# Token lists of experts 12 to 31 read from a table in DRAM, empty slots left out of the scatter-add, four more ring places ahead of the expert loop, another order in the last norm

## What is computed

```python
logits = xt @ w_router + b_router
top_val, top_idx = lax.top_k(logits, TOP_K)          # TOP_K = 4 of 32
gate_w = jax.nn.softmax(top_val, axis=-1)
h = clamped_swiglu(xe @ w_gate[e] + b_gate[e], xe @ w_up[e] + b_up[e])
y = h @ w_down[e] + b_down[e]                        # for the tokens of expert e
out = zeros.at[token].add(y * gate_w)
x2 = layer_norm(DEEPNORM_ALPHA * x1 + out, ln2_g, ln2_b)
```

## Time and profile before

| | us |
|---|---|
| median of 3 runs | 1449.98 |
| lowest, highest | 1448.16, 1451.69 |
| the profiled execution | 1448.46 |
| its span | 1445.9 |

### The profile page before, as it was taken

One profiled execution on the slowest core, in us unless ns is written; L12 is line 12 of the kernel. 1 busy time (PEld: TensorE's weight loads), 2 busy tenths in 40 slices (PEclk: granted clock), 3 DMA queues, 4 the chain that ended last, 5 costly groups with the idle time before them and its releaser, 6 DMA issues.

```text
span 1445.9 us, 37854 instructions
## 1 busy us (share of the span) xinstructions
PE 1390.0 (96%) x16642; PEld 939.8 (65%) x16642; DVE 468.0 (32%) x891; ACT 325.3 (22%) x669; POOL 116.1 (8%) x122
## 2 busy tenths in 40 slices
PE   7999999998999999999999999999999999999991
PEld 6767776565566666666666666666666666666660
DVE  3335665374323222222222223222222222222224
ACT  4544566131111111111121111111111121111114
POOL 1022000001100000000000000000000001000000
PEclk9999999998999999999999999999999999999995
DMA  8211041727999999999999999999999999999964
GB/s 264 74 49 59 1 151 63 272 102 295 404 394 397 400 392 397 399 400 397 402 399 398 394 392 400 398 398 386 396 397 392 400 391 400 391 392 389 395 269 145
DMA packets 78565, 463.94 MB, mean 321 GB/s; under 512 B 12449, under 2 KB 13745, under 8 KB 29105
## 3 DMA queue, kind: packets, MB, share of 16 engines
q1 hardware_dynamic: 67616, 429.54, 74.3%
q0 software_dynamic: 10288, 31.32, 8.4%
q10 hardware_dynamic: 512, 0.79, 0.1%
HBM read 444.70 MB, written 22.22 MB: 323 GB/s over the span
## 4 chain that ended last, share of the span: by engine, by line
PE 88%; DVE 5%; DMA 3%; ACT 3%; issue 1%; DVEq 0%; SPq 0%; ACTq 0%; POOLq 0%
PE unit L1255 41%; PE unit L1258 26%; PE unit L1159 4%; PE unit L1238 2%; DMA ring_b<-w_down_dram 2%; PE unit L758 2%; PE unit L1243 2%; PE unit L760 2%; PE unit L759 2%; PE unit L753 1%; PE unit L886 1%; DVE attT L2184 1%; PE unit L910 1%; PE unit L793 1%; PE unit L1232 0%
## 5 line engine op out<-in xcount | busy, mean ns | idle before, releaser
L1255 PE MATMUL unit<-ring_b,xeT 128*32 128x512 f32 (+1 forms) x3168 | 353.9, 489 | 1.1 <-ACT xeT L1418 1.1
L1258 PE MATMUL unit<-ring_b,xeT 128*32 128x256 f32 x1584 | 354.5, 381 | 0.0
L1258 PE MATMUL unit<-ring_a,xeT 128*32 128x256 f32 x1488 | 330.7, 379 | 0.0
L1255 PE MATMUL unit<-ring_a,xeT 128*32 128x256 f32 (+1 forms) x2976 | 330.2, 486 | 0.0
L1258 PEld LDWEIGHTS unit<-ring_b,xeT 128*32 128x32 f32 x1584 | 171.5, 110 | 56.5 <-issue 1.0
L1258 PEld LDWEIGHTS unit<-ring_a,xeT 128*32 128x32 f32 x1488 | 161.8, 110 | 52.5
L1255 PE MATMUL unit<-ring_a,heT 128*32 128x512 f32 (+1 forms) x1536 | 169.6, 486 | 0.5 <-DMA ring_a<-w_down_dram 0.5
L1258 PE MATMUL unit<-ring_a,heT 128*32 128x256 f32 x768 | 169.9, 379 | 0.0
L1255 PEld LDWEIGHTS unit<-ring_b,xeT 128*32 128x32 f32 x3168 | 126.5, 110 | 60.8 <-issue 4.5
L1255 PE MATMUL unit<-ring_b,heT 128*32 128x256 f32 (+1 forms) x1440 | 160.1, 486 | 0.5 <-DMA ring_b<-w_down_dram 0.5
L1258 PE MATMUL unit<-ring_b,heT 128*32 128x256 f32 x720 | 160.3, 379 | 0.0
(11 more groups left out here) (325 smaller groups left out, 1592.2 us busy)
## 6 DMA issues: line engine op xcount, KB each, us to landing
ring_b<-w_gate_dram SPq DMA_DIRECT2D x68, 1024.0 KB, 28.3
ring_a<-w_down_dram SPq DMA_DIRECT2D x68, 1024.0 KB, 29.6
ring_b<-w_up_dram SPq DMA_DIRECT2D x64, 1024.0 KB, 29.9
ring_a<-w_up_dram SPq DMA_DIRECT2D x64, 1024.0 KB, 30.4
ring_a<-w_gate_dram SPq DMA_DIRECT2D x60, 1024.0 KB, 29.0
ring_b<-w_down_dram SPq DMA_DIRECT2D x60, 1024.0 KB, 28.7
raw_a<-w_in_dram SPq DMA_DIRECT2D x16, 512.0 KB, 3.6
wo<-w_out_dram SPq DMA_DIRECT2D x2, 1024.0 KB, 7.5
```

The costliest lines, as they stand in the source:

```text
L1255: return mm(out[j * NS:(j + 1) * NS, a:b], stat(j), w[:, a:b], start=first, stop=last)
L1258: return mm(out[CAP:P, j * 256:(j + 1) * 256], stat(j), w[:, FOLD:D], start=start, stop=stop)
```

## The change

- `idx` gets a column for each expert. Experts 0 to 11 have their row numbers made as before, without DVE's wait for `y_free`. For experts 12 to 31 `pick_rows`, `rows_of` and `read_rows` are gone.
- A DRAM tensor `lists` takes their place. At the start it is filled with numbers from 544 up (`no_rows`). DVE works out once, from `onehot`, `posm` and the expert numbers `idxfs`, where each of a token's four entries belongs (`place`). These eight instructions stand ahead of the first bias shuffle.
- POOL writes the entries with 20 scatters of up to 128 single 4-byte numbers: three behind each of the steps 0 to 5 and two behind step 6. Behind step 7 it reads the columns of experts 12 to 31 into `idx` in one DMA.
- The scatter-add has the bound that the gathers have, so that empty slots are left out. `acc_rows` shrinks to 544 rows, and the early copy from `w_gate` is gone.
- SP waits for the first gather ahead of place 12 instead of place 8.
- ACT takes the sum of tile 1 ahead of the root of tile 0.
- The decay of the sample state waits for `go4` instead of a semaphore of its own.

```diff
-        idx = sb("idx", [P, TURN], I32)
+        idx = sb("idx", [P, NE], I32)
...
+        lists_dram = nc.dram_tensor("lists", (CAP * NE + NT * P * TOPK, 1), I32, kind="Internal").ap()
+        acc_dram = nc.dram_tensor("acc_rows", (T, D), F32, kind="Internal").ap()
...
                     if m == 8:
                         sp.wait_ge(*filled("out3"))
+                    if m == 12:
                         sp.wait_ge(x1_ready, NT)
                         sp.wait_ge(x_rows, 16)
...
-            pool.dma_start(acc_dram[T:XROWS], d["w_gate"][0, 0, 0:P]).then_inc(out_done, 16)
...
-                                               compute_op=ALU.add)
+                                               bounds_check=T - 1, oob_is_err=False, compute_op=ALU.add)
+            def enter(some):
+
+                pool.wait_ge(mask_ready, NT + 2)
+                for i, k in some:
+                    r = rows(i)
+                    pool.indirect_dma_start(lists_dram, bass.IndirectOffsetOnAxis(ap=place[:r, i, k:k + 1], axis=0),
+                                            tokid[:r, i:i + 1], None).then_inc(out_done, 16)
...
+            for e in range(LISTED - 2):
+                pool_step(e, e == 0)
+                enter(entries[e * 3:(e + 1) * 3])
+                if e == 7:
+                    pool.wait_ge(out_done, 16 * (OUTS + NT * TOPK))
+                    pool.dma_start(idx[:CAP, LISTED:NE], lists_dram[0:CAP * NE].rearrange("(s e) a -> s (e a)", e=NE)
+                                   [:, LISTED:NE]).then_inc(lists_in, 16)
...
-                if not no_more:
+                if e + 2 < LISTED:
                     pe.wait_ge(picked, e + 3)
                     pe.wait_ge(gate_read, e + 2)
                     rows_of(tok_done, CAP)
...
-            act.wait_ge(s_read, 1)
+            act.wait_ge(*filled("go4"))
...
+            st(tt(onehot[:], onehot[:], posm[:].unsqueeze(2).to_broadcast([P, NT, TOPK, NE]), ALU.mult))
+            tokv = k_("tokv").rearrange("p (t c) -> p t c", c=3)
+            st(tt(tokid[:], tokv[:, :, 0], tokv[:, :, 1], ALU.add))
+            st.settle()
+            st(red(placef[:], onehot[:], ALU.add))
+            st.settle()
+            st(ts(over[:], placef[:], float(CAP), None, ALU.is_ge))
+            st(stt(placef[:], placef[:], float(NE), idxfs[:], ALU.mult, ALU.add))
+            st.settle()
+            spill = k_("spill").rearrange("p (t k) -> p t k", k=TOPK)
+            st(tt(onehot[:, :, :, 0], spill, placef[:], ALU.subtract))
+            st.settle()
+            st(tt(over[:], over[:], onehot[:, :, :, 0], ALU.mult))
+            st.settle()
+            st(tt(place[:], placef[:], over[:], ALU.add))
+            st.settle()
+            v.sem_inc(mask_ready, 1)
             over_partitions(0, 0, gate_bias_in)
             read_rows(1, 1)
```

More of the change, by code:

```diff
@@ L312, in build @@
         xpos = sb("xpos", [P, NT])
+        tokid = sb("tokid", [P, NT], I32)
+        place = sb("place", [P, NT, TOPK], I32)
+        placef = sb("placef", [P, NT, TOPK])
+        over = sb("over", [P, NT, TOPK])
         assert here[0] <= qkv_at + 2 * D * 4
@@ L659, in gather @@
             def gather(n):
-                at = idx[:CAP, n % TURN:n % TURN + 1]
+                at = idx[:CAP, n:n + 1]
                 pool.indirect_dma_start(xg[:CAP], None, x1_dram, bass.IndirectOffsetOnAxis(ap=at, axis=0),
@@ L705, in pool_step @@
                     pool.sem_inc(turn_over, 1)
-                    gather(par + 2)
+                    gather(e + 2)
                 if first:
@@ L2269, in _ @@
             st(nc.vector.memset(msk[:], 0.0))
+            st(nc.vector.memset(idxfs[:], 0.0))
             st.settle()
@@ L2488, in _ @@
             dve_step(0, 0)
-            for e in range(1, TURN):
-                dve_step(e, e)
-            with v.Fori(1, NE // TURN - 1) as it:
+            for e in range(1, 3 * TURN):
+                dve_step(e, e % TURN)
+            with v.Fori(3, NE // TURN - 1) as it:
                 for par in range(TURN):
```

86 lines of the change are left out of this document (44 added, 42 removed).

## The result

| | before | after |
|---|---|---|
| median of 5 runs | 1448.16 | 1459.48 |
| lowest, highest | 1446.88, 1451.69 | 1456.03, 1462.51 |
| the profiled execution | 1448.46 | 1462.51 |
| its span | 1445.9 | 1460.2 |

The changed kernel is slower, by less than 1%: ratio 1.0063, 95% interval 1.0042 to 1.0084; the medians lie 11.3 us apart. The forecast of 1447.2 and its range up to 1455 were wrong.

The account below looks back on a forecast made before the run. PE was taken to bound the loop, with the DMAs about 2% behind. Terms -3.6 + 1.6 - 1.4 - 0.5 + 1.1 = -2.8 us gave 1445.7 from the profiled execution, 1447.2 us carried to the median; range 1442.5 to 1455.

Parts of the forecast that it names:

- What bounds the kernel: Expert loop: PE bounds it, the DMAs are about 2% from doing it and lose 0.67 us per expert against PE.
- Row numbers out of the steps: Steps e = 10 to 29: five matmuls fewer save 0.18 us in each of 20 steps, -3.6 us.
- Rival 1: Row-number matmuls are worth their full busy time: the loop gains 7.0 us in place of 3.6, 1443.8; chance 0.17.
- The block ahead of the loop: Start: eight new DVE instructions delay PE's first product by +1.6 us, bounds 1.0 to 2.5.
- Four more places: Weight ring: places 8 to 11 issued earlier give 11.2 us of reserve and remove two late waits, -1.4 us.
- Rows of empty slots: Scatter-add: dropped rows save at most 0.49 us of DMA time per expert; last add -0.5 us (0 to -1.0).
- The scatters: POOL's queue in early steps: no time lost, 0 us, but 10 us taken off the DMA reserve.
- rival 3: Scatters hold POOL's queue and the gather behind them is late; at 4 us per scatter +15.6, 1463; chance 0.14.
- The last norm: End, on ACT: the table load now stands in line, so DVE ends later, +1.1 us (0.4 to 1.5).
- The reserve at the end: DMA reserve of weights at the loop's end: 12 us, or -2 with nothing gained from the dropped rows.
- rival 4: Late steps: scatters and entries use up the reserve and the DMAs fall behind, +2.2 us, 1452.2 or more; chance 0.06.

Follow-up runs that it names:

- b_ring: The kernel before with one edit: SP waits for the first gather ahead of ring place 12 in place of 8; 1448.44 us, ratio 0.9986.
- b_bound: The kernel before with a bound on the scatter-add, so that empty slots are left out; 1451.65 us, ratio 1.0005.
- the spread: Slots reordered so empty ones fall on all engines; tried on the kernel before with the scatter-add's bound: 1451.21 us, ratio 0.9985.
- b_shift64: The kernel before with an unused tile of 64 bytes per partition behind the constants, moving nearly all later tiles; 1459.64 us against 1452.22, ratio 1.0051.
- a_pad192: The changed kernel with an unused tile of 192 bytes, so that ring_a, xg and ysb start at a multiple of 256; 1449.34 us, ratio 0.9988.
- a_best2: Changed kernel with spread slots, ring_b at 128, 64-byte tile, old norm order, later DVE block, two scatters behind each of steps 0 to 9; 1455.79 us, ratio 1.0020.

## Why the prediction was wrong, step by step

- **What bounds the kernel.** Right. Landing times gave 0.67 us per expert that the DMAs lose against PE; the slowest engine's pace gives 34.20 - 33.48 = 0.72.
- **Row numbers out of the steps.** Right: 0.19 us for each of 20 steps, 3.8 for 3.6. Rival 1 falls.
- **The block ahead of the loop.** 1.7 us for 1.6 on the way to the first product (the forecast's own terms, 2.77 - 1.26, add up to 1.5). With the clock it was 2.45 in one profile and 0.8 in the other, within the bounds of 1.0 to 2.5 or just below, which had named the clock.
- **Four more places.** Right: b_ring loses both late waits. The last large row store lands in 5.9 to 8.0 us beside the weights in place of 3.0, and still ahead of the first gather, so it costs nothing.
- **Rows of empty slots.** The first step that failed. 0.49 us of DMA time per expert was an average over 16 engines, and the text itself said of the last add "if some engines still have six full rows, nothing". It did not carry that over to the weights. Eleven engines keep their six rows, and the pace stays, 34.3 for 34.2. In the last add the bound alone gave nothing (9.72 us from its issue to the first statistics in b_bound, 9.25 before, 9.4 to 10.0 in the changed kernel and its variants); with the spread it is 8.8 to 9.2. Term: -0.5 forecast, +0.1 to +0.7 measured.
- **The tiles' places.** The second step that failed, by being absent. The sum had no term for where tiles lie, though the diff shows `KEEP` growing by 20 numbers, ahead of everything. It costs 0.3 us per expert, 7.4 us of time in b_shift64.
- **The scatters.** Their POOL time (0.97 to 1.03 us each) and the gather behind them were judged rightly, and rival 3 did not happen. The queue term was of the right size: 35.0 to 35.6 us per expert while they run in place of 34.4, so some 0.8 x 7 = 6 us of reserve, where 10 were taken. That was luck in part. The forecast counted 8 packets and a signal on each engine; on record a scatter is one packet of 32 bytes there, 15 ns, and a signal, 9 ns, which does not add up to the 0.3 us that each one costs the weights. What was missed is that PE itself slows behind three in a row, 7 to 8 us in most of the profiles. **This is the third step that failed:** the scatters were judged by POOL's queue and the DMAs alone, and their price on PE was put at nothing.
- **The last norm.** +0.87 for +1.1, by the mechanism forecast.
- **The reserve at the end.** 19.5 + 11.2, less ten experts at 34.5 - 33.48 = 1.0 and nineteen at 34.5 - 33.29 = 1.2, less 6 for the scatters, is -8 us. The forecast had 12, or -2 in the worst case. Measured are 11.6 us lost in the last ten steps, of which 8.3 stand in the rows of waits. So **rival 4** is what happened. It was given a chance of 0.06 and a price of at least 1452.2 from one cause, the scatters' entries. The cause that counted was the pace of the loads: the forecast had only a gain of 0.49 or 0 for it, and the runs showed a loss of 0.3 us per expert. The -8 is an estimate, and that it comes so near to 8.3 is luck too.

## What to carry to other kernels

Where a loop lives on DMAs, look at the slowest of the engines, not at bytes or at their mean share: work left out must come off the engine that is last, so deal empty slots out over all engines. Any edit that changes the size of an early tile moves all later ones; compare offsets modulo 256 before and after, and where the targets of the big loads lay at a multiple of 256, keep them there. Small scatters issued in a row can slow an engine that does not touch them, and 10 us between them was enough here.

## What the runs showed of the hardware that was not expected

- 64 bytes of shift of the tiles slow the slowest DMA engine from 34.2 to 34.5 us per expert (12.6 MB of weights, one add and one gather of 96 rows), 128 do the same, and back at a multiple of 256 it is 34.2. The median packet of 8192 bytes goes from 309 to 313 ns with it.
- The 16 engines of a queue drift apart until the signals of one load lie 21 to 25 us from first to last, and no further. In the kernel before, ten or eleven earlier loads have then not fully landed at each issue (8 early in the loop, and 12 at most in any profile looked at). A new load lands on the first engine some 7 us after its issue and on the last 28 to 31 us after it. That fits first engines that have run out of loads, while the queue goes at the slowest one's pace. With evenly dealt rows they stay within 2 to 4 us in the kernels with the longer head start.
- A scatter of 128 numbers of 4 bytes is one packet of 32 bytes on each of the 16 engines. Three of them, 1.3 us apart, cost PE 1.1 us on average, in the middle of a product, with no wait on record but "issue", in all but two of the profiles that had three in a row (the first of after, and a_pad192). What sets those two apart is not known.
- A wait of PE of 5.0 us inside the loop (a_best2) brought 6.8 us at the lower of the two clock levels.
